# A two-layer decoder on one core: the order of weight preparation in the Strassen pairs, an input tile ahead of the memory jobs, and more attention steps in the first half of an output part

## The chip, the cores and the metric

The kernel runs on one core of a Trainium2 chip. The metric is the device time of one execution in microseconds (us), here the median of three runs; less is better.

## What is computed

A decoder trunk of two layers over x (1024 positions by D = 1024), with a memory of 256 rows. Cut to what matters:

```python
for l in range(2):
    h = rms_norm(x, norm_gains[l, 0])
    z = h @ w_in[l]                              # 768 main + 256 memory columns
    if l == 0:
        y_main = pool_mixer(z[..., :768], w_pool[l], pool_scale[l])
    else:
        y_main = dilated_mixer(z[..., :768], positions, shared)   # 3 groups of 4 heads, softmax over groups
    y_mem = memory_attn(z[..., 768:], mem, mem_norm[l], w_mem_kv[l])
    y = jnp.concatenate([y_main, y_mem], axis=-1) @ w_out[l]
    x = x + rms_norm(y, norm_gains[l, 1])
    h = rms_norm(x, norm_gains[l, 2])
    gu = h @ w_gate_up[l]                        # 2 x 2816 columns
    x = x + rms_norm((silu(gu[..., :2816]) * gu[..., 2816:]) @ w_down[l], norm_gains[l, 3])
    if l == 0:
        shared = build_shared_kv(x, positions, kv_norm, w_kv)
```

`pool_mixer` averages over windows of 2, 4, 8 and 16 positions and multiplies by `w_pool`; `memory_attn` has 4 heads over the 256 memory rows; `dilated_mixer` is a sliding window of 128 keys at dilations 1, 4 and 16. All inputs are float32.

## The kernel before

**Arithmetic.** Every float32 product is three matmuls: each operand is split into a high part (`..H`, a rounding copy on ACT) and a low part (`..L`, the difference, on DVE or POOL), and TensorE adds high x high, low x high and high x low. Activations lie with D on the partitions, in 8 tiles (k) of 128, and the 1024 positions are two halves of 512, so a typical matmul is 128x512.

**Jobs.** `plan_jobs` (L106) lists the jobs in TensorE's order: per layer `in` (input tiles), `mem` (keys and values of the memory), `pool` or `kv`, `out`, `ffn` (the first 4 of 22 hidden tiles, by halves), `st` (the other 18, a **pair** each of a gate and an up tile, computed with 7 Strassen-Winograd products of 4 k x 3 = 12 matmuls, 84 in all), and `down` (32). `region` gives each job's weights a slot in SBUF, `banks` its PSUM banks. A weight comes by a DMA on SP's queue, which issues in order (L2461), gets its gain and high part (`weight_hi`, L1004, ACT) and its low part (`weight_lo`, L1578 on DVE, L2347 on POOL).

**Queues.** Each engine's instruction order is written out by hand in one function per engine and tied together by semaphores: a wait holds all that stands behind it on that engine. Steps of attention (scores L803, transposes L787, values L777 on TensorE; exp L1111, normalising L1117 on ACT; several on DVE) are laid between the matmuls of jobs at the k that `HOOKS` names. Sums over D for the norms are TensorE steps `("col", s, h)` (L688, column sum of squares) and `("row", s, h)` (L697, spread of the inverse root to all partitions); `("mcol",)`, `("mrow",)` are the memory's, `("mv", l, a)` its value transposes (L741, copied by ACT at L1087).

**Pairs.** For pair q, DMA brings four raw tiles into `SR` (1 MB); DVE (layer 0, `st_add`, L1877 to L1880) or POOL (layer 1, L2429 to L2432) forms four sums. ACT makes high parts of the raw tiles (`st_raw_hi`, L1252) and of the sums (`st_sum_hi`, L1257) in `SH`, DVE the low parts `SL` (L1887, L1894). Between these, DVE combines the products of the running pair (u2 L1900, c11 L1906, u3 L1911, L1917 and L1918, c21 L1922, c12 L1927, L1950) and ACT does `p1_copy` (L1279) and silu (L1263 after c11, L1269 after c12). `pe.wait_ge(st_lo, 2 * (q + 1))` opens each pair.

**Weights prepared in advance.** During the first 16 pairs of layer 0, 24 later weights are prepared and written back to HBM: one or two per pair, `prepared(f)` L163. SP loads `VR` (L2469), ACT scales it by its gains and copies its high part (`keep_weight`, L1141, L1144), POOL makes the low part `VL` (L2390), SP writes `w_keep` (L2476, L2479). ACT's part of a pair in layer 0:

```python
p1_copy(q)
if l == 0:
    silu_first(q)
    for i in prepared(f):
        keep_weight(i)
if f < NF - 1:
    st_raw_hi(q + 1)
    st_sum_hi(q + 1)
```

**Other places.** In layer 1, `out` is done in two parts of four k (part 0 beside the last attention steps). The three groups' outputs are weighted against each other per pair of head tiles: `combine(0)`, `combine(1)` on ACT (L1490 to L1496), `combine_last` on DVE, low parts by `split_low` (L1814). Part 1 is added onto part 0 by `add_y` (L1848); `residual` (L1630) adds the input, after y was multiplied by its inverse root: for y of layer 1's mixer this multiplication is POOL's `y_norm` (L2422). Then come x's squares (`accumulate`, L1613), `BH`, `BL` (L1641 low), and `scale_x` (L1075).

## Time and profile before

| what | value |
|---|---|
| three runs | 2398.61, 2398.93, 2392.47 us; median 2398.61 |
| the profiled execution's own time | 2402.4 us |
| its span in the profile | 2400.4 us |
| mean clock that TensorE was granted | 0.955 of full speed |
| instructions | 25623, of which TensorE 9718 matmuls |
| chain that ended last | PE 70%, DVE 12%, ACT 9%, issue 5%, DMA 3% |

A row of a timeline gives an instruction's start, its length, engine, line, operation with tiles as out<-in, and in brackets how long the engine was idle before it and what released it. A waits row names the engine and line that waited, and for whose result. PE is TensorE, PEld its weight loads, DVE VectorE, ACT ScalarE, POOL GpSimd, SPq the queue of DMAs that SyncE issues.

### The profile page before, as it was taken

The page shows a single profiled execution, that of the slowest core. Times are in us where ns is not written, and L with a number is a line of the kernel's source. Part 1 is how long each engine was busy: PE and PEld are TensorE (multiplying, and loading weights), DVE is VectorE, ACT ScalarE, POOL GpSimd, SP SyncE. Part 2 cuts the span into 40 slices and gives each one's busy share as a digit, 9 for nine tenths or more (in the row PEclk, how much of TensorE's full clock was granted, in tenths as well). Part 3 has the DMA queues.
Part 4 walks back from the last instruction along what each step waited for, and adds up shares of the span by engine and source line. Part 5 has one row for each costly group of instructions (what it writes and reads, how often), then busy time and mean ns, then how long its engine had stood idle before and what let it go on. Part 6 is the DMA issues. An engine that isn't in the chain of part 4 may idle for free.

```text
span 2400.4 us, 25623 instructions
## 1 busy us (share of the span) xinstructions
PE 2202.2 (92%) x9718; PEld 1766.8 (74%) x9718; DVE 1264.6 (53%) x1901; ACT 944.5 (39%) x1575; POOL 328.0 (14%) x198
## 2 busy tenths in 40 slices
PE   6897999888888999998999997979799999999996
PEld 5675888776767778887777765657578888878885
DVE  6354375655565643525344445466656666672442
ACT  5335352434344433322444446653542222242421
POOL 3432100112111000000000014022222222200000
PEclk8998999999899999998999999989899999999998
DMA  4202232344444635554111101004212222263543
GB/s 160 73 14 90 88 121 75 142 184 149 179 148 173 222 117 199 163 174 182 53 64 43 59 30 36 19 17 154 75 53 79 79 79 82 94 216 97 197 132 104
DMA packets 83210, 265.10 MB, mean 110 GB/s; under 512 B 9360, under 2 KB 10640, under 8 KB 77840
## 3 DMA queue, kind: packets, MB, share of 16 engines
q1 hardware_dynamic: 66960, 234.10, 27.8%
q10 hardware_dynamic: 16128, 29.37, 3.6%
q8 instruction: 77, 1.26, 0.2%
q14 instruction: 45, 0.37, 0.0%
HBM read 195.14 MB, written 68.29 MB: 110 GB/s over the span
## 4 chain that ended last, share of the span: by engine, by line
PE 70%; DVE 12%; ACT 9%; issue 5%; DMA 3%; SPq 1%; POOL 0%; ACTq 0%; DVEq 0%
PE PS L662 8%; PE PS L875 7%; PE PS L877 7%; PE PS L876 7%; PE PS L663 7%; PE PS L665 7%; PE PS L895 6%; PE PS L897 6%; PE PS L896 6%; PE PSC L803 3%; ACT VR L1141 2%; PE PO L777 2%; DVE SL L1894 2%; PE PTR L787 1%; ACT VH L1144 1%
## 5 line engine op out<-in xcount | busy, mean ns | idle before, releaser
L895 PE MATMUL PS<-IH,DH 128*128 128x512 f32 x704 | 276.6, 393 | 6.5 <-DVE IL L1975 6.0
L897 PE MATMUL PS<-IH,DL 128*128 128x512 f32 x704 | 275.3, 391 | 0.0
L896 PE MATMUL PS<-IL,DH 128*128 128x512 f32 x704 | 275.3, 391 | 0.0
L875 PE MATMUL PS<-BH,SH 128*128 128x512 f32 x432 | 179.1, 415 | 54.7 <-DVE SL L1894 51.6
L875 PE MATMUL PS<-BHT,SH 128*128 128x512 f32 x576 | 225.8, 392 | 0.0
L876 PE MATMUL PS<-BLT,SH 128*128 128x512 f32 x576 | 224.2, 389 | 0.0
L877 PE MATMUL PS<-BHT,SL 128*128 128x512 f32 x576 | 224.2, 389 | 0.0
L876 PE MATMUL PS<-BL,SH 128*128 128x512 f32 x432 | 176.7, 409 | 0.0
L877 PE MATMUL PS<-BH,SL 128*128 128x512 f32 x432 | 176.7, 409 | 0.0
L895 PEld LDWEIGHTS PS<-IH,DH 128*128 128x128 f32 x704 | 132.9, 189 | 36.7 <-DVE IL L1975 8.5
L897 PEld LDWEIGHTS PS<-IH,DL 128*128 128x128 f32 x704 | 133.0, 189 | 27.9
L896 PEld LDWEIGHTS PS<-IL,DH 128*128 128x128 f32 x704 | 133.0, 189 | 27.5
L875 PEld LDWEIGHTS PS<-BH,SH 128*128 128x128 f32 x432 | 85.8, 199 | 79.6 <-DVE SL L1894 61.8
L1578 DVE TENSOR_TENSOR DL<-DR,DH 128x1408 fp32r<-128x1408 f32 x64 | 103.8, 1624 | 73.0 <-ACT DH L1004 73.0
L662 PE MATMUL PS<-XH,WH 128*128 128x512 f32 x320 | 138.8, 434 | 0.0
L663 PE MATMUL PS<-XL,WH 128*128 128x512 f32 x320 | 128.7, 402 | 0.0
L875 PEld LDWEIGHTS PS<-BHT,SH 128*128 128x128 f32 x576 | 109.4, 190 | 23.0
L876 PEld LDWEIGHTS PS<-BLT,SH 128*128 128x128 f32 x576 | 109.4, 190 | 23.0
L1613 DVE TENSOR_TENSOR SS<-SS,SCR 128x512 f32<-128x512 f32 x28 | 19.4, 691 | 202.6 <-ACT SCR L1031 202.6
L877 PEld LDWEIGHTS PS<-BHT,SL 128*128 128x128 f32 x576 | 108.1, 188 | 23.0
L662 PE MATMUL PS<-BH,WH 128*128 128x512 f32 x256 | 104.7, 409 | 20.9 <-DVE WL L1578 13.4
L2390 POOL TENSOR_TENSOR VL<-VR,VH 128x1024 fp32r<-128x1024 f32 x24 | 57.9, 2411 | 470.4 <-ACT VH L1144 470.4
(281 smaller groups left out, 4645.2 us busy)
## 6 DMA issues: line engine op xcount, KB each, us to landing
DR<-in_wdn SPq DMA_DIRECT2D x64, 704.0 KB, 4.1
SR<-in_wst SPq DMA_DIRECT2D x36, 1024.0 KB, 4.8
IR<-inner SPq DMA_DIRECT2D x88, 256.0 KB, 4.9
WR<-in_w SPq DMA_DIRECT2D x36, 512.0 KB, 4.6
inner<-TP SPq DMA_DIRECT2D x36, 512.0 KB, 2.6
VR<-in_w SPq DMA_DIRECT2D x24, 512.0 KB, 4.1
w_keep<-VH SPq DMA_DIRECT2D x24, 512.0 KB, 3.7
w_keep<-VL SPq DMA_DIRECT2D x24, 512.0 KB, 4.6
```

Source lines behind the costliest of these rows:

```text
L662: MM(out[h], wh[:, i, :], rh(h, k), start=(i == 0), stop=False)
L663: MM(out[h], wh[:, i, :], rl(h, k), start=False, stop=False)
L665: ins = MM(out[h], wl[:, i, :], rh(h, k), start=False, stop=last)
L803: MM(score_bank(a)[:, 0:nk], QF[rows, t, P * n:P * (n + 1)], keys, start=True, stop=True).then_inc(scored, 1)
L875: MM(BANK[bank], SH[b][:, w, c], BH[t][:, k, :], start=(k == 0), stop=False)
L876: MM(BANK[bank], SH[b][:, w, c], BL[t][:, k, :], start=False, stop=False)
L877: ins = MM(BANK[bank], SL[b][:, w, c], BH[t][:, k, :], start=False, stop=(k == 3))
L895: MM(bank, wh[:, i, :], IH[r][:, :], start=(k == 0), stop=False)
L896: MM(bank, wh[:, i, :], IL[r][:, :], start=False, stop=False)
L897: ins = MM(bank, wl[:, i, :], IH[r][:, :], start=False, stop=(k == NF - 1))
L1578: V.tensor_tensor(lo(j), raw(j), as_f32(hi(j)), ALU.subtract).then_inc(w_lo_dve, 1)
L2390: G_.tensor_tensor(VL[i % NV][:, :, :], VR[i % NV][:, :, :], as_f32(VH[i % NV][:, :, :]), ALU.subtract).then_inc(v_lo, 1)
```

## The change

- **Opening, layer 0.** The job `in` of tile `POOL_IN[0]` = 3 stands ahead of the four `mem` jobs on TensorE, in the loads and in the preparation of weights, and holds PSUM banks 4 and 5; the `mem` jobs take banks 6, 0, 1, 6. The column and row steps of the first norm lie in it (k = 3, 4 and 7), `mcol` and `mrow` in the memory jobs 0 and 1. SP loads weights only up to job `mem` 3 before it writes `mem_keep` (L2597). ACT squares x before it touches the memory. The later input jobs have 4, 5, 5, 5, 5 steps for 4 each in six.
- **Pairs, layer 0.** ACT's order becomes p1_copy, first `keep_weight`, `st_raw_hi`, `silu_first`, `st_sum_hi`, second `keep_weight`.
- **Junction.** `RSTDM` is reloaded at down job 13; the transposes of memory values lie in the job `in` 7 of half 1 (k = 6) rather than half 0 (k = 4).
- **Attention and out part 0, layer 1.** Four steps in each of the 8 jobs of the first half, one in each of the second (before: 21 and 19). `combine` on ACT is cut into single pieces, and `combine(1)` with `combine_last` stands earlier.
- **Residual and FFN start, layer 1.** `y_norm` leaves POOL, DVE does the multiplication inside `residual`. The `ffn` weights have slots of their own (`2 * f + j`), in space that part 0 of `out` used, and are prepared earlier. `("col", s_x, 1)`, `("row", s_x, 1)` lie in `ffn` job (1, 0, 0) at k = 0 and 4 rather than in (1, 0, 1) at 3 and 7.
- Slots of layer 1's pairs and down jobs are counted from the other parity (`pair_slot`).

```diff
+            run += [Job("in", 0, POOL_IN[0])]
             run += [Job("mem", 0, m, gain=8) for m in range(4)]
-            run += [Job("in", 0, m) for m in POOL_IN]
+            run += [Job("in", 0, m) for m in POOL_IN[1:]]
...
-        jobs += [Job("ffn", l, (f, j), halves=(h,), tag=h, slot=wide(2 * f + j),
+        jobs += [Job("ffn", l, (f, j), halves=(h,), tag=h, slot=2 * f + j if l else wide(2 * f + j),
...
-            HOOKS[J[("out", 1, m, (0, 0))]] = (1, 2, 3) if m < 5 else (1, 3)
-            HOOKS[J[("out", 1, m, (0, 1))]] = (0, 1, 2, 3) if m < 2 else (1, 3) if m < 7 else (1,)
+            HOOKS[J[("out", 1, m, (0, 0))]] = (0, 1, 2, 3)
+            HOOKS[J[("out", 1, m, (0, 1))]] = (1,)
...
-            memory_job(0, 0, hook=at_k({6: [("col", 0, 0), ("col", 0, 1)]}))
-            memory_job(0, 1, hook=at_k({4: [("row", 0, 0), ("row", 0, 1)], 7: [("mcol", 0, 0)]}))
-            memory_job(0, 2, hook=at_k({6: [("mrow", 0, 0)]}))
+            job(J[("in", 0, POOL_IN[0], None)], xh, xl,
+                hook=at_k({3: [("col", 0, 0)], 4: [("col", 0, 1)], 7: [("row", 0, 0), ("row", 0, 1)]}))
+            memory_job(0, 0, hook=at_k({1: [("mcol", 0, 0)]}))
+            memory_job(0, 1, hook=at_k({3: [("mrow", 0, 0)]}))
+            memory_job(0, 2)
             memory_job(0, 3)
...
-                              (1, 0, 1): {3: [("col", s_x, 1)], 7: [("row", s_x, 1)]}}
+                              (1, 0, 0): {0: [("col", s_x, 1)], 4: [("row", s_x, 1)]}}
...
                     p1_copy(q)
+                    ready = prepared(f) if l == 0 else ()
+                    if len(ready):
+                        keep_weight(ready[0])
+                    if f < NF - 1:
+                        st_raw_hi(q + 1)
                     if l == 0:
                         silu_first(q)
-                        for i in prepared(f):
-                            keep_weight(i)
                     if f < NF - 1:
-                        st_raw_hi(q + 1)
                         st_sum_hi(q + 1)
+                    if len(ready) > 1:
+                        keep_weight(ready[1])
...
-                if r != 3:
-                    V.tensor_tensor(y, y, RSTD[:, c], ALU.mult).then_inc(y_normed[h], 1)
+                V.tensor_tensor(y, y, RSTD[:, c], ALU.mult).then_inc(y_normed[h], 1)
...
-                    if h and m >= 2:
-                        combine_last(m - 2)
+                    if (h, m) == (0, 7):
+                        combine_last(0)
+                        combine_last(1)
+                    if h and m in (1, 2, 4, 6):
+                        combine_last((2, 3, 4, 5)[(1, 2, 4, 6).index(m)])
+                    if h and m == 7:
+                        combine_last(6)
+                        combine_last(7)
+                        split_low(7, 22)
...
-            y_norm(0)
-            y_norm(1)
...
-            loads_to(J[("in", 0, POOL_IN[2], None)])
+            loads_to(J[("in", 0, POOL_IN[1], None)])
```

**The order in a layer-0 pair on ACT**, one with two preparations (`VR`, `VH` are the weight being prepared, `SR`, `SH` raw tiles, sums and their high parts, `SCR` p1). Before:

```order
L1279 ACTIVATE SCR_71<-PS 128x512 [waits c21_done,st_mm]
L1263 ACTIVATE TP_91<-TP_91 128x512 [waits c11_done]
L1141 ACTIVATE VR_192<-VR_192,GN 128x128 [waits v_loaded1]
L1141 ACTIVATE VR_192<-VR_192,GN 128x128 x7
L1144 ACTIVATE VH_198<-VR_192 128x1024 [waits v_gained]
L1141 ACTIVATE VR_193<-VR_193,GN 128x128 [waits v_loaded2]
L1141 ACTIVATE VR_193<-VR_193,GN 128x128 x7
L1144 ACTIVATE VH_199<-VR_193 128x1024 [waits v_gained]
L1252 ACTIVATE SH_204<-SR_200 128x1536 [waits st_loaded0]
L1257 ACTIVATE SH_204<-SR_200 128x2048 [waits st_added]
L1269 ACTIVATE TP_91<-TP_91 128x512 [waits c12_done]
```

After:

```order
L1293 ACTIVATE SCR_71<-PS 128x512 [waits c21_done,st_mm]
L1154 ACTIVATE VR_192<-VR_192,GN 128x128 [waits v_loaded1]
L1154 ACTIVATE VR_192<-VR_192,GN 128x128 x7
L1157 ACTIVATE VH_198<-VR_192 128x1024 [waits v_gained]
L1266 ACTIVATE SH_204<-SR_200 128x1536 [waits st_loaded0]
L1277 ACTIVATE TP_91<-TP_91 128x512 [waits c11_done]
L1271 ACTIVATE SH_204<-SR_200 128x2048 [waits st_added]
L1154 ACTIVATE VR_193<-VR_193,GN 128x128 [waits v_loaded2]
L1154 ACTIVATE VR_193<-VR_193,GN 128x128 x7
L1157 ACTIVATE VH_199<-VR_193 128x1024 [waits v_gained]
L1283 ACTIVATE TP_91<-TP_91 128x512 [waits c12_done]
```

The first preparation and the raw conversion (128x1536) moved ahead of the silu that waits for c11, the second preparation behind the conversion of the sums (128x2048).

**The opening on TensorE**, around the first column sum (`SS` squares, `XHA` x's high part, `MH` the memory's). Before, it lies in a memory job:

```order
L729 MATMUL PSC<-ML_64,WH_167 128x256
L730 MATMUL PSC<-MH_66,WL_141 128x256
L688 MATMUL PX<-CN,SS 128x1 [waits ss0_done]
L688 MATMUL PX<-CN,SS 128x1 x3
L688 MATMUL PX<-CN,SS 128x1 [waits px_free,ss0_done]
L688 MATMUL PX<-CN,SS 128x1 x3
L728 MATMUL PSC<-MH_66,WH_167 128x256
L729 MATMUL PSC<-ML_64,WH_167 128x256
L730 MATMUL PSC<-MH_66,WL_141 128x256
L728 MATMUL PTR<-MH_66,WH_168 128x256 [waits w_lo_pool]
```

After, it lies in the inserted input job, between its matmuls:

```order
L672 MATMUL PSC<-XHA,WL_141 128x512
L672 MATMUL PTR<-XHA,WL_141 128x512
L695 MATMUL PX<-CN,SS 128x1 [waits ss0_done]
L695 MATMUL PX<-CN,SS 128x1 x3
L669 MATMUL PSC<-XHA,WH_167 128x512
L670 MATMUL PSC<-XLA,WH_167 128x512
L669 MATMUL PTR<-XHA,WH_167 128x512
L670 MATMUL PTR<-XLA,WH_167 128x512
L672 MATMUL PSC<-XHA,WL_141 128x512
```

**Layer 1's mixer residual on DVE**, first half (`YOA` is y, `WL` a low part of an `ffn` weight). Before:

```order
L1848 TENSOR_TENSOR YOA<-YOA,PO 128x512 [waits mm_done,y_first]
L1630 SCALAR_TENSOR_TENSOR YOA<-YOA,GN,TP_91 128x512 [waits x_back0,y_normed0]
L1641 SCALAR_TENSOR_TENSOR BL_229<-YOA,GN,BH_221 128x512 [waits x_hi0]
L1630 SCALAR_TENSOR_TENSOR YOA<-YOA,GN,TP_91 128x512 [waits x_back1,y_normed0]
L1641 SCALAR_TENSOR_TENSOR BL_229<-YOA,GN,BH_221 128x512 [waits x_hi0]
L1848 TENSOR_TENSOR YOA<-YOA,PS 128x512 [waits mm_done,y_first]
L1578 TENSOR_TENSOR WL_143<-WR_117,WH_169 128x1024 [waits w_hi]
L1630 SCALAR_TENSOR_TENSOR YOA<-YOA,GN,TP_92 128x512 [waits x_back2,y_normed0]
L1641 SCALAR_TENSOR_TENSOR BL_230<-YOA,GN,BH_222 128x512 [waits x_hi0]
L1630 SCALAR_TENSOR_TENSOR YOA<-YOA,GN,TP_91 128x512 [waits x_back0,y_normed0]
L1641 SCALAR_TENSOR_TENSOR BL_230<-YOA,GN,BH_222 128x512 [waits x_hi0]
```

After:

```order
L1606 RECIPROCAL RC<-RC 128x4 [waits px_free]
L1601 TENSOR_TENSOR WL_142<-WR_116,WH_168 128x1024 [waits w_hi]
L1881 TENSOR_TENSOR YOA<-YOA,PTR 128x512 [waits mm_done,y_first]
L1648 TENSOR_TENSOR YOA<-YOA,RSTD 128x512 [waits px_free]
L1652 SCALAR_TENSOR_TENSOR YOA<-YOA,GN,TP_91 128x512 [waits x_back0,y_normed0]
L1648 TENSOR_TENSOR YOA<-YOA,RSTD 128x512
L1652 SCALAR_TENSOR_TENSOR YOA<-YOA,GN,TP_91 128x512 [waits x_back1,y_normed0]
L1663 SCALAR_TENSOR_TENSOR BL_229<-YOA,GN,BH_221 128x512 [waits x_hi0]
L1648 TENSOR_TENSOR YOA<-YOA,RSTD 128x512
L1652 SCALAR_TENSOR_TENSOR YOA<-YOA,GN,TP_92 128x512 [waits x_back2,y_normed0]
L1663 SCALAR_TENSOR_TENSOR BL_229<-YOA,GN,BH_221 128x512 [waits x_hi0]
```

Each L1652 (before L1630) has a multiplication by `RSTD` ahead of it on DVE, and the low parts of weights have left the stretch.

## Rows read from the trace of the kernel before

**Rows 1.** the page's busy us (share of the span) xinstructions

```profile
PE 2202.2 (92%) x9718; PEld 1766.8 (74%) x9718; DVE 1264.6 (53%) x1901; ACT 944.5 (39%) x1575; POOL 328.0 (14%) x198
```

**Rows 2.** what TensorE waited for, whole span: us in total, times, longest

```profile
PE PS L875 <- DVE SL L1894: 51.6, 16, 4.9
PE PO L777 <- ACT PT L1111: 22.1, 9, 7.2
PE PS L662 <- DVE WL L1578: 13.4, 3, 9.9
PE PS L662 <- DVE CL L1814: 11.1, 2, 8.9
PE PX L688 <- DVE SS L1605: 7.0, 1, 7.0
PE PSC L803 <- ACT VM L1087: 5.9, 1, 5.9
PE PX L741 <- DVE MV L1692: 4.7, 1, 4.7
```

**Rows 3.** windows: length, busy us of PE PEld DVE ACT POOL; PEclk, DMA, GB/s

```profile
412.36:791.64 379.28, 327.71 (x1346) 264.30 (x1344) 211.39 (x238) 161.73 (x295) 57.86 (x24) 0.94 0.44 163
1807.42:2110.00 302.58, 302.58 (x1336) 250.56 (x1335) 191.37 (x191) 81.03 (x68) 82.63 (x64) 1.00 0.24 87
44.58:72.44 27.86, 20.08 (x121) 18.69 (x122) 8.56 (x12) 7.83 (x13) 10.21 (x5) 0.81 0.45 156
1668.67:1788.31 119.64, 96.49 (x403) 76.85 (x403) 80.06 (x84) 59.26 (x80) 20.07 (x12) 0.91 0.23 81
```

**Rows 4.** timeline, two pair starts: start, us, engine, line, operation [idle <- releaser]

```profile
433.07 0.50 PE L875 MATMUL PS<-BH,SH 128*128 128x512 f32 x1 [1.50 <-DVE SL L1894]
457.33 0.79 PE L875 MATMUL PS<-BH,SH 128*128 128x512 f32 x1 [4.93 <-DVE SL L1894]
```

**Rows 5.** timeline of ACT in the pair from 433.07, which has two weight preparations

```profile
436.12 0.60 ACT L1279 ACTIVATE SCR<-PS 128x512 f32<-128x512 f32 x1 [0.45 <-PE PS L877]
...
442.82 2.44 ACT L1141 ACTIVATE VR<-VR,GN 128x128 f32<-128x128 f32 x8
...
449.69 1.47 ACT L1252 ACTIVATE SH<-SR 128x1536 fp32r<-128x1536 f32 x1
451.06 1.90 ACT L1257 ACTIVATE SH<-SR 128x2048 fp32r<-128x2048 f32 x1
```

**Rows 6.** DVE in the same pair; L1887 over the kernel (ns, min/median/max)

```profile
441.56 0.69 DVE L1906 TENSOR_TENSOR TP<-SCR,PS 128x512 f32<-128x512 f32 x1 [2.03 <-PE PS L877]
...
455.00 2.28 DVE L1894 TENSOR_TENSOR SL<-SR,SH 128x2048 fp32r<-128x2048 f32 x1
...
L1887 DVE TENSOR_TENSOR SL<-SR,SH x36: 1750/1756/2700, 399.0 to 2107.4; 128x1536 fp32r<-128x1536 f32 x36
```

**Rows 7.** `VL` on POOL, `VR` loads on SP's queue, their us to landing

```profile
425.58 2.41 POOL L2390 TENSOR_TENSOR VL<-VR,VH 128x1024 fp32r<-128x1024 f32 x1 [167.29 <-ACT VH L1144]
...
466.62 3.23 SPq L2469 DMA_DIRECT2D VR<-in_w  x2
...
VR<-in_w SPq DMA_DIRECT2D x24, 512.0 KB, 4.1
```

**Rows 8.** opening: SP's first write of memory, ACT's weight behind it

```profile
59.67 0.33 SPq L2597 DMA_DIRECT2D mem_keep<-MH  x1
...
70.76 1.06 ACT L1004 ACTIVATE WH<-WR 128x1024 fp32r<-128x1024 f32 x1 [9.29 <-DMA WR<-in_w]
```

**Rows 9.** residual and y_norm over the kernel: ns min/median/max, first and last start

```profile
L1630 DVE SCALAR_TENSOR_TENSOR YOA<-YOA,GN,TP x32: 741/752/1780, 282.4 to 1724.4; 128x512 f32<-128x512 f32 x32
...
L2422 POOL TENSOR_TENSOR YOA<-YOA,RSTD x16: 1282/1726/1747, 1647.1 to 1711.7; 128x512 f32<-128x512 f32 x16
```

**Rows 10.** timeline, layer 1's FFN start: ACT's scalings, TensorE's column sum

```profile
1729.86 5.00 ACT L1075 ACTIVATE YOA<-YOA,GN 128x512 f32<-128x512 f32 x8
...
1744.03 0.94 PE L688 MATMUL PX<-CN,SS 128*128 128x1 f32 x8
```

More of the change, by code:

```diff
@@ L594, in build @@
         HOOKS = {}
-        for m in range(NMT):
-            HOOKS[J[("in", 0, m, None)]] = (1, 3, 5, 7)
+        for n, m in enumerate(POOL_IN):
+            HOOKS[J[("in", 0, m, None)]] = () if n == 0 else (4, 5, 6, 7) if n == 1 else (1, 2, 4, 5, 7)
         first_stage_job = J[("kv", 1, stage_tile(0), None)]
@@ L827, in _, with hook @@
                 j = J[("in", 0, m, None)]
-                def hook(i, first=n == 0, places=HOOKS[j]):
-                    if first and i == 0:
+                if n == 0:
+                    continue
+                def hook(i, first=n == 1, places=HOOKS[j]):
+                    if first and i == 2:
                         memory_values(0, 0)
@@ L1163, in _ @@
                     weight_hi(1)
+            weight_hi(2)
+            for k in range(KT):
+                square0(k)
             act.wait_ge(tables_in, MEM_IN)
@@ L1190, in _ @@
                 j = J[("in", 0, m, None)]
-                if n == 0:
+                if n == 1:
                     memory_values(0)
-                ahead(j)
+                if n:
+                    ahead(j)
                 for _ in HOOKS[j]:
@@ L1462, in _ @@
             sub_layer(0)
-            for k in range(6):
-                residual(2, 1, k)
-            memory_values(1)
-            for k in range(6, KT):
+            for k in range(KT):
                 residual(2, 1, k)
@@ L1471, in _ @@
             norm_row(4, 1)
+            memory_values(1)
             for k in range(4, KT):
@@ L1478, in swap_quarter, with combine @@
                 A(T[1][r:r + 32, :], PS[j % 2][q:q + 32, :], ACT.Copy).then_inc(swapped, 1)
-            def combine(pair, stage):
+            def combine(pair, stage, g=None):
                 tiles = [2 * g + pair for g in range(3)]
-                if stage == 0:
-                    for g, t in enumerate(tiles):
-                        act.wait_ge(cmb_diff, 3 * pair + g + 1)
-                        A(QF[:, t, :], QF[:, t, :], ACT.Exp).then_inc(cmb_exp, 1)
-                elif stage == 1:
+                if stage == "exp":
+                    act.wait_ge(cmb_diff, 3 * pair + g + 1)
+                    A(QF[:, tiles[g], :], QF[:, tiles[g], :], ACT.Exp).then_inc(cmb_exp, 1)
+                elif stage == "inverse":
                     tmp = MX[:, :] if pair == 0 else T[3]
@@ L1493, in combine @@
                 else:
-                    for g, t in enumerate(tiles):
-                        act.wait_ge(cmb_out, 3 * pair + g + 1)
-                        A(CH[:, t, :], OF[:, t, :], ACT.Copy).then_inc(c_hi, 1)
+                    act.wait_ge(cmb_out, 3 * pair + g + 1)
+                    A(CH[:, tiles[g], :], OF[:, tiles[g], :], ACT.Copy).then_inc(c_hi, 1)
             def split_memory(m):
@@ L1765, in _, with pooled_input @@
             query0(7)
+            def pooled_input(n):
+                j = J[("in", 0, POOL_IN[n], None)]
+                dve.wait_ge(mm_done, j + 1)
+                if n == 0:
+                    dve.wait_ge(pads_zero, 3)
+                    for h in range(2):
+                        ins = V.tensor_tensor(T[0][:, HALF[h]], BANK[banks(j)[h]], RSTD[:, HALF[h]], ALU.mult)
+                    ins.then_inc(in_scaled, 1)
+                else:
+                    V.tensor_tensor(T[0], PS[j % 2][:, :], RSTD[:, :], ALU.mult).then_inc(in_scaled, 1)
+            pooled_input(0)
             for m in range(4):
@@ L2274, in combine_last @@
                 else:
-                    for n, t in enumerate(tiles):
-                        split_low(t, 18 + n + 1)
-                    split_low(7, 22)
+                    split_low(tiles[part - 5], 18 + part - 4)
             for n in range(19):
@@ L2362, in _ @@
             pool.wait_ge(x0_lo, KT)
-            gain(POOL_JOBS[0])
-            weights_to(first + 3)
+            weight_lo(POOL_JOBS[0])
+            done[0] += 1
+            pool.wait_ge(ss0_done, KT)
+            gain(POOL_JOBS[1])
+            weights_to(J[("in", 0, POOL_IN[3], None)])
             pool.wait_ge(pads_zero, 3)
@@ L2416, in _ @@
             weights_to(NJ)
-            def y_norm(h):
-                pool.wait_ge(px_free, px_at[("row", 5, h)])
-                for k in range(KT):
-                    G_.tensor_tensor(YO[h][:, k, :], YO[h][:, k, :], RSTD[:, HALF[h]],
-                                     ALU.mult).then_inc(y_normed[h], 1)
             def st_add(q):
-                b = SR[q % 2]
+                b = SR[pair_slot(q)]
                 pool.wait_ge(*st_seen(q))
```

117 lines of the change are left out of this document (61 added, 56 removed).

## The prediction

> **What bounds the kernel now.** I read the page's head and busy shares first: one TensorE, busy 2202.2 us, 92% of the span, and no other engine that computes over 53% [rows 1]. So the time is TensorE's matmuls, plus TensorE's idle time, plus what its lower clock costs behind each idle stretch. The next view is therefore the list of what TensorE waited for [rows 2]: the first line is one wait, 16 times, before L875, the first matmul of a Strassen pair, for L1894, DVE's low part of the eight sums (`SL`). It is 51.6 us in all; the next one, attention's 22.1 for `PT`, is less than half of it. The third view prices it: the 16 pair starts of layer 0 are spread over 379.28 us, TensorE idle for 51.6 of them and its clock at 0.94; the layer-1 pairs run in 302.58 us with no idle time at clock 1.00 [rows 3]. There 1336 matmuls take 302.58 us, 0.2265 us each, so a pair of 84 matmuls takes **19.02 us** where nothing stops it; in layer 0 it takes 379.28 / 16 = **23.70 us**.
>
> Why is `SL` late? The timelines of one pair show it, T = 433.07 its first matmul [rows 4 to 6]. ACT copies p1 at T+3.05 and then waits for DVE's c11 (T+8.49) to do silu. Only behind that come two weight preparations (`keep_weight`, 442.82 to 449.69, 3.43 each), then the conversions of the next pair's raw tiles (1.37 until the next one starts) and of its sums (1.90). DVE takes the low parts behind these, the last of them L1894 from T+21.93 to T+24.21, and the next pair starts at T+24.26, after 4.93 of idle time. A pair with one preparation ends the same chain one preparation sooner, and its successor waits 1.50 [rows 4]; eight of each make 51.4.
>
> **Term by term, against the profiled execution (2402.4 us, 3.8 above the runs' median of 2398.61).**
>
> *Pairs (ACT's order).* One preparation and the raw conversion move in front of silu, into the time in which ACT idled for c11; the second preparation goes behind the sum conversion. In the same pair: p1 copied by T+3.65, first preparation to T+7.1, raw conversion to T+8.5 (ACT never waits for its DMA now), c11 ends T+9.2, silu some 0.6 later. DVE makes the sums in four operations (to T+12.0 at c11's 0.69 each) and forms u3 until T+12.6, then L1887 (1.75 unhindered) to T+14.3. ACT's sum conversion goes from T+12.0 to T+13.9. DVE's two sums of products, then L1894 (2.28): `SL` is done at T+17.8. It is wanted at T+19.02, a reserve of 1.2. If nothing is late, 16 x (23.70 − 19.02) = 74.9 goes, of which 51.6 is idle time and 23.3 slow clock (1.46 a pair). Moved too: POOL's low part `VL` of the first preparation, 2.41 long, now begins at T+7.1 rather than at T+13.2 (425.58, in a pair that starts at 412.36), and `w_keep`'s writes with it. L1887 shows what company costs: 2700 against a median of 1756 ns [rows 6, 7]. Add that 0.95 to the chain and it ends at T+18.7, still 0.3 early. I take **−73**; bounds −74.9 (all) and −58 (a gap near 1 us stays in every pair).
>
> By the Trainium skill ("SBUF — State Buffer", section "SBUF: two separate sides") a DVE operation with two SBUF inputs and a GpSimd operation share a port pair as an exclusive lock, held for the whole instruction. The long L1887 agrees in direction, since it lost 0.95 beside `VL`. By that page a DVE operation could lose up to a whole `VL`, 2.41, and then `SL` ends at T+20.2 and 1.2 a pair stays: 19 us less gain. That is rival 1's mechanism.
>
> *Opening (an input job ahead of the memory jobs).* From the column sum that waited 7.0 for DVE's `SS` to the first memory scores that waited 5.9 for `VM`, 27.86 us pass with TensorE busy 20.08 at clock 0.81 [rows 2, 3]. The inserted job gives DVE and ACT its length of 48 matmuls: both waits go (12.9), with 1.9 of smaller gaps (27.86 − 20.08 − 5.9) and 5.3 of slow clock (0.19 x 27.86): 20. New is that the next job's weight lies behind the three writes of memory on SP's queue: now from the first write at 59.67 to ACT's use of the weight at 70.76 it is 11.1 us, and ACT idles 9.29 for it [rows 8]. With the write at about 57.3 (an estimate: the memory's row step is reached 2.4 sooner) the weight lands at 68.4, high part 1.1 and low part 2.4 behind; TensorE is out of prepared work at about 64.5 and idles 7.5, plus 1.6 of clock. Row steps that now stand close behind their column steps cost about 2.2. Together 20 − 11.3, **−8** rounded down; bounds −3 and −12.
>
> *Junction.* The transposes of memory values wait 4.7 for `MV` [rows 2]; they move a half job later. The column sum that follows them is then waited for instead, about half of it: **−2.5**; bounds 0 and −8. The reload of rstd goes to an idle queue place and is costed at nothing; its cover is the down jobs.
>
> *Attention and out part 0.* Thirty-two steps instead of 21 lie in the first half, eight in the second, so the combination of pair 1 is ready before part 1 asks for it. The wait for `CL` (11.1 in two) goes, and 1.4 of clock as behind a pair's gap: **−12.5**; bounds −5 (the shorter spacing of the steps gives some back as waits for `PT`, which is 22.1 already) and −17. Combination 0 in single pieces between steps shortens some of those 22.1: **−2**; bounds 0 and −5.
>
> *Residual and FFN start, layer 1.* From 1668.67 to 1788.31, 119.64 us, all that is not matmul at full clock is at most 119.64 − 403 x 0.2265 = 28.3 (23.2 idle, 5.2 slow clock in the 96.49 busy) [rows 3]. It is the three waits for L1578's `WL` (13.4 [rows 2]) and smaller ones. The weights of the FFN are prepared earlier because out part 0's space is free, so `WL` is no wait. POOL's y_norm (16, median 1726 ns [rows 9]) becomes 16 DVE operations of some 0.75 (no row shows it on DVE; L1630 of that width has median 752 ns): 12 us more of DVE, but POOL no longer stretches L1630 up to 1780. What is late next: the column sum of y's second half, 2.4 (bounds 0 and 6.0, eight such operations); the column sum of x's second half, which waited for nothing at 1744.03 [rows 10] and is now asked 33 matmuls (7.5 us) earlier, 6.0 (0 and 7.5); its row sum behind ACT's eight scalings of 5.00 [rows 10], 3.4 (0 and 5.0). 28.3 − 11.8: **−16.5**; bounds −8 and −24. Slot numbers of layer 1's pairs and down jobs only change parity: nothing.
>
> Sum: −73 − 8 − 2.5 − 12.5 − 2 − 16.5 = −114.5, so 2287.9 for a profiled run, and on the median **2284 us**.
>
> **Rivals.** *1. Half of the pair gain.* The early `VL` or the silu/c11 interlock leaves the eight two-preparation pairs where one-preparation pairs stand now: 1.5 + 1.46 each, 8 x 2.96 = 23.7. For it: the reserve of only 0.3 to 1.2. Against: layer 1's pairs have the same chain without preparations and no gap. **2307**, chance 0.13. *2. Only the pairs gain.* Outside them each removed wait is taken over by another (weight behind `mem_keep`, `PT`, column sums); 39.0 of the gain (8 + 14.5 + 16.5) is void: **2323**, chance 0.07. *3. More goes.* The waits that I added (11.8 at the FFN, about 8 of the opening's 11.3) do not come about: **2264**, chance 0.09. *4. Slower.* The preparation now stands ahead of the raw conversion, so ACT's wait for its weight `VR` holds the next pair. The two loads issue at 466.62, that is 9.3 after their pair's start, for 3.23, and land 4.1 later [rows 7]: T+16.6. They are used in the next pair, at T+19.0 + 3.65 = T+22.7, and 1.2 of reserve stands behind. The rival decides from a landing at about T+31, 14.5 us later, where 7.2 idle a pair (16 x 7.2 = 115) eats the whole gain; at 8.3 a pair it is 2284 + 16 x 8.3 = **2417**. Only 44% of the DMA time is used there [rows 3]: chance 0.02.
>
> **Numbers.** Forecast 0.68, the rest as above, 0.01 unnamed. The range 2262 to 2310 holds the forecast with its bounds, rival 3 and rival 1; rival 2 and 4 lie outside. Changes within 0.3% (7 us) are what this measurement can't tell from none; every case but rival 4 lies far below: faster 0.97, same 0.01, slower 0.02.
>
> **What would show it.** Right: no line L875 <- `SL` in the waits, pairs of 19.0 us at clock 1.00 in layer 0; ACT's second preparation behind the sum conversion; the opening's `SS` and `VM` waits gone, and one of some 7 us for a low weight part in their place; layer 1's pairs start some 114 us sooner, since every term lies ahead of them. Wrong: gaps of 1 us or more at the pairs with two preparations (rival 1), new waits in the place of those for `CL` and `WL`, as long as they were (rival 2), or idle time of ACT before `VR` (rival 4).

## The result, and the profile after

The changed kernel takes **2282.39 us** (median of four runs, 2281.26 to 2292.21) against 2397.72 us before (four runs): a ratio of 0.9532, 95% interval 0.9502 to 0.9562. The forecast was 2284. The profiled execution took 2281.26 us, with a span of 2278.9 us, against 2402.4 and 2400.4.

The head of the page, busy us and share of the span by engine:

```profile
PE 2158.3 (95%) x9718; PEld 1738.4 (76%) x9718; DVE 1254.2 (55%) x1918; ACT 947.2 (42%) x1575; POOL 303.9 (13%) x182
```

TensorE lost 122 us of span and 44 us of busy time (2202.2 in [rows 1]): most of what went was idle time, the rest is the same 9718 matmuls taking less time each. What TensorE waits for now (us in total, times, longest):

```profile
PE PO L784 <- ACT PT L1124: 22.7, 9, 7.2
PE PTR L794 <- DVE PR L1744: 17.7, 13, 2.5
PE PX L695 <- DVE SS L1636: 13.8, 5, 4.9
PE PS L669 <- POOL WL L2381: 7.6, 2, 6.5
PE PS L669 <- DVE CL L1847: 2.4, 3, 1.6
PE PS L888 <- DVE SL L1927: 0.6, 1, 0.6
```

Against [rows 2]: `SL` is down from 51.6 to 0.6; `CL` of `split_low` (L1814 before, L1847 now) is down from 11.1 to 2.4; `WL` on DVE (13.4), `SS` in the opening (7.0), `VM` (5.9) and `MV` (4.7) are gone. New is `WL` on POOL, 6.5 of it in the opening. Up are `SS` of L1636, the sums of squares of later norms, from 1.9 in two to 13.8 in five, and `PR` from 13.6 in eleven to 17.7 in thirteen. The two stretches of pairs, layer 0 and layer 1 (length, busy us of PE, PEld, DVE, ACT, POOL, then PEclk, DMA share, GB/s):

```profile
409.16:753.43 344.27, 343.17 (x1513) 283.55 (x1512) 239.68 (x273) 182.65 (x324) 58.15 (x24) 1.00 0.57 209
1669.61:2012.43 342.82, 342.82 (x1512) 283.87 (x1513) 219.60 (x224) 96.08 (x88) 87.94 (x68) 1.00 0.27 98
```

Eighteen pairs in 344.27 and in 342.82 us, 19.1 and 19.0 each, at clock 1.00 in both layers [rows 3 for before]. ACT, DVE and POOL in the pair that starts at 467.20 and has two preparations:

```profile
470.12 0.60 ACT L1293 ACTIVATE SCR<-PS 128x512 f32<-128x512 f32 x1 [1.36 <-PE PS L890]
470.61 2.44 ACT L1154 ACTIVATE VR<-VR,GN 128x128 f32<-128x128 f32 x8
...
474.04 1.47 ACT L1266 ACTIVATE SH<-SR 128x1536 fp32r<-128x1536 f32 x1
476.28 0.63 ACT L1277 ACTIVATE TP<-TP 128x512 f32<-128x512 f32 x1 [0.76 <-DVE TP L1939]
479.39 1.92 ACT L1271 ACTIVATE SH<-SR 128x2048 fp32r<-128x2048 f32 x1 [2.48 <-DVE SR L1913]
481.21 2.44 ACT L1154 ACTIVATE VR<-VR,GN 128x128 f32<-128x128 f32 x8
```

```profile
475.56 0.69 DVE L1939 TENSOR_TENSOR TP<-SCR,PS 128x512 f32<-128x512 f32 x1 [2.03 <-PE PS L890]
476.16 1.01 DVE L1910 TENSOR_TENSOR SR<-SR 128x512 f32<-128x512 f32 x1
...
479.87 1.75 DVE L1920 TENSOR_TENSOR SL<-SR,SH 128x1536 fp32r<-128x1536 f32 x1
...
482.73 2.28 DVE L1927 TENSOR_TENSOR SL<-SR,SH 128x2048 fp32r<-128x2048 f32 x1
...
485.75 2.08 DVE L1983 TENSOR_TENSOR TP<-TP,TP 128x512 f32<-128x512 f32 x1
```

```profile
474.22 2.41 POOL L2427 TENSOR_TENSOR VL<-VR,VH 128x1024 fp32r<-128x1024 f32 x1 [16.63 <-ACT VH L1157]
484.82 2.45 POOL L2427 TENSOR_TENSOR VL<-VR,VH 128x1024 fp32r<-128x1024 f32 x1 [8.20 <-ACT VH L1157]
```

This is the chain of the forecast, with T = 467.20: preparation 1 from p1's end, raw conversion at T+6.8, silu behind c11, sum conversion at T+12.2, L1927 done at 485.01 = T+17.8, where the forecast had T+17.8. The next pair starts at 486.24, 19.04 after T.

Cut by TensorE's marks in the timelines, the two profiled executions and those of experiments 2, 1, 8 and 11 stand so (us; "to the PT wait" ends at the 5 us wait for `PT` ahead of the out part, [rows 2, 22.1 in all]):

| stretch | before | after | new pair order alone | old pair order | old attention steps | late weights |
|---|---|---|---|---|---|---|
| up to layer 0's pairs | 412.4 | 409.2 | 410.5 | 411.8 | 410.2 | 410.6 |
| its pairs | 420.8 | 344.2 | 344.3 | 421.0 | 344.3 | 344.3 |
| its down jobs | 251.7 | 251.1 | 252.7 | 251.2 | 252.4 | 252.9 |
| layer 1 to the PT wait | 413.7 | 402.6 | 407.2 | 403.6 | 407.7 | 407.4 |
| to layer 1's pairs | 289.7 | 262.4 | 289.6 | 262.7 | 272.9 | 288.3 |
| its pairs | 345.5 | 342.8 | 345.6 | 342.8 | 342.8 | 344.7 |
| the rest | 266.6 | 266.5 | 265.8 | 265.7 | 266.1 | 266.3 |

### The profile page after: what moved, and what is told of

The parts are those of the page before. It is cut to its first block, busy times and chain, and to the rows that moved or that the text cites. A ratio compares the mean times of both kernels' runs of the same rounds, so it can differ in the third digit from the quotient of the medians.

```text
span 2278.9 us, 25627 instructions
## 1 busy us (share of the span) xinstructions
PE 2158.3 (95%) x9718; PEld 1738.4 (76%) x9718; DVE 1254.2 (55%) x1918; ACT 947.2 (42%) x1575; POOL 303.9 (13%) x182
## 4 chain that ended last, share of the span: by engine, by line
PE 81%; DVE 8%; ACT 4%; DMA 3%; issue 3%; SPq 0%; POOL 0%; ACTq 0%; DVEq 0%
PE PS L890 9%; PE PS L888 9%; PE PS L889 9%; PE PS L669 8%; PE PS L670 8%; PE PS L672 7%; PE PS L908 7%; PE PS L909 6%; PE PS L910 6%; PE PSC L812 3%; PE PO L784 2%; PE PTR L794 1%; DMA TP<-x_mid 1%; DVE SS L1636 1%; DVE IL L2008 1%
## 5 line engine op out<-in xcount | busy, mean ns | idle before, releaser
L888 PE MATMUL PS<-BH,SH 128*128 128x512 f32 x432 | 168.3, 389 | 0.6 <-DVE SL L1927 0.6
L889 PE MATMUL PS<-BL,SH 128*128 128x512 f32 x432 | 168.1, 389 | 0.0
L890 PE MATMUL PS<-BH,SL 128*128 128x512 f32 x432 | 168.0, 389 | 0.0
L1636 DVE TENSOR_TENSOR SS<-SS,SCR 128x512 f32<-128x512 f32 x28 | 19.4, 691 | 202.5 <-ACT SCR L1044 202.5
L1734 DVE CUSTOM_DVE_ANT_0 PSC<-PSC,MK 128x128 f32<-128x128 f32 (+1 forms) x88 | 32.2, 366 | 157.1 <-PE PSC L812 156.9
L1271 ACT ACTIVATE SH<-SR 128x2048 fp32r<-128x2048 f32 x36 | 69.1, 1920 | 107.8 <-POOL SR L2462 67.9
```

The source lines that it names most:

```text
L888: MM(BANK[bank], SH[b][:, w, c], BH[t][:, k, :], start=(k == 0), stop=False)
L889: MM(BANK[bank], SH[b][:, w, c], BL[t][:, k, :], start=False, stop=False)
L890: ins = MM(BANK[bank], SL[b][:, w, c], BH[t][:, k, :], start=False, stop=(k == 3))
L1271: A(SH[pair_slot(q)][:, S3:, :], SR[pair_slot(q)][:, S3:, :], ACT.Copy).then_inc(st_hi, 1)
```

## The experiments

**1. The old pair order in the changed kernel.** ACT's part of a pair only:

```diff
-                    ready = prepared(f) if l == 0 else ()
-                    if len(ready):
-                        keep_weight(ready[0])
-                    if f < NF - 1:
-                        st_raw_hi(q + 1)
                     if l == 0:
                         silu_first(q)
+                        for i in prepared(f):
+                            keep_weight(i)
                     if f < NF - 1:
+                        st_raw_hi(q + 1)
                         st_sum_hi(q + 1)
-                    if len(ready) > 1:
-                        keep_weight(ready[1])
```

> The changed kernel with ACT's old order in the layer-0 pairs (silu, all weight preparations, raw conversion, sum conversion), nothing else undone. Theory (this order alone makes SL late): the gaps of 1.5 and 4.9 us in front of L888 come back at 16 pairs, with the slow clock behind them, some 76 us: about 2358 us. Rival (the pairs are freed by other parts too, such as the slots or the opening): clearly less comes back, 2300 to 2340, with gaps of another size.

Measured: 2359.84 us (2357.46 to 2363.29), 77.5 more than the changed kernel. The list of waits has the old row back, with the same numbers:

```profile
PE PS L888 <- DVE SL L1923: 51.6, 16, 4.9
```

**2. The new pair order alone in the kernel before** (the same edit the other way round).

> The kernel before with the new ACT order in the layer-0 pairs and nothing else of the change. Theory: 76 us go, 2398 - 76 = about 2322 us, and the other parts keep their waits (SS 7.0, VM 5.9, CL 11.1, WL 13.4). Rival (parts depend on each other): less than 65 us go.

Measured: 2319.84 us (2315.84 to 2324.16) against 2396.46, 76.6 less. The other stretches are those of before within 2 us, but for the one to the PT wait, 407.2 against 413.7 (below). Undone and done alone give the same size, so the pairs' gain depends on no other part.

**3. Silu ahead of the first preparation.** Only the second preparation keeps its new place:

```diff
+                    if l == 0:
+                        silu_first(q)
                     if len(ready):
                         keep_weight(ready[0])
                     if f < NF - 1:
                         st_raw_hi(q + 1)
-                    if l == 0:
-                        silu_first(q)
-                    if f < NF - 1:
                         st_sum_hi(q + 1)
```

> The changed kernel, but with silu ahead of the first preparation: p1 copy, silu, preparation 1, raw conversion, sum conversion, preparation 2. Only the second preparation is still moved. Chain theory: c11 ends at T+9.0, preparation 1 at T+13.1, raw conversion T+14.6, DVE's L1920 behind POOL's VL until about T+17.3, L1927 until about T+20.5: each of the 16 pairs waits about 1.5 us as a one-preparation pair did before, and with 1.46 of slow clock each it is 16 x 2.96 = 47 us more, about 2329 us. Rival (only two preparations in a row hurt, one does not): no gap, 2282 us.

Measured: 2309.27 us (2305.34 to 2309.98), 26.9 more than the changed kernel and 20 less than the 2329 expected. The waits row, the window of one pair of it, and for comparison two pairs of the kernel before, the first behind a wait of 1.50 and the second behind one of 4.93 (the last three numbers are PEclk, DMA share, GB/s; each window ends with the wait of the next pair):

```profile
PE PS L888 <- DVE SL L1926: 24.1, 16, 1.5
```

```profile
453.00:473.83 20.83, 19.33 (x84) 15.69 (x84) 14.69 (x16) 8.34 (x14) 4.60 (x2) 1.00 0.66 230
```

```profile
433.07:457.33 24.26, 19.33 (x84) 15.69 (x84) 13.32 (x16) 11.85 (x23) 4.81 (x2) 0.97 0.46 170
457.33:480.74 23.41, 21.91 (x85) 17.57 (x85) 13.33 (x16) 8.45 (x14) 2.41 (x1) 0.88 0.47 162
```

The gap is the 1.5 us of the chain, 16 times: that theory stands. The slow clock behind it does not exist: a pair takes 19.33 busy us at clock 1.00 behind a gap of 1.50 (0.3 over 19.02, what stopping and starting costs TensorE), and 21.91 at 0.88 behind one of 4.93. The timeline of the kernel before shows the clock in the matmuls' spacing:

```profile
458.35 0.63 PE L877 MATMUL PS<-BH,SL 128*128 128x512 f32 x1
458.78 0.63 PE L875 MATMUL PS<-BH,SH 128*128 128x512 f32 x1
...
463.18 0.39 PE L877 MATMUL PS<-BHT,SL 128*128 128x512 f32 x1
463.41 0.40 PE L875 MATMUL PS<-BHT,SH 128*128 128x512 f32 x1
```

Behind the gap of 4.93 the starts are 0.43 apart until 462.62, then 0.23: the lower and the higher of the two levels (1.2 and 2.4 GHz), 13 matmuls at 0.2 us more each. So of the 23.3 us that I had put down to the clock, 7 long gaps in that window made 7 x 2.58 = 18, and the stops and starts 16 x 0.3 = 5; the short gaps cost no clock.

The second preparation's move alone thus gives about two thirds of the gain, 50 of 77 us, and the work put ahead of silu the other 27.

**4. Both preparations ahead of the raw conversion.**

```diff
-                    if len(ready):
-                        keep_weight(ready[0])
+                    for i in ready:
+                        keep_weight(i)
...
-                    if len(ready) > 1:
-                        keep_weight(ready[1])
```

> The changed kernel, but with both preparations ahead of the raw conversion. By ACT's chain alone (preparations to T+10.5, raw conversion T+12.0, sum conversion behind the sums at T+12.0) SL is still ready at T+17.8: 2282 us, no gap. If POOL's VL blocks a two-input DVE operation until VL ends, the second VL (T+10.6 to T+13.0) holds DVE's sums until about T+13.9, and SL is ready at about T+19.5: gaps near 0.5 us at the 8 pairs behind two preparations, with slow clock 10 to 16 us more, 2292 to 2298 us.

Measured: 2292.44 us (2289.90 to 2294.12), 10 more; in the profile the pairs take 352.8 us against 344.3. POOL's second `VL`, DVE's second and third sum, and the waits:

```profile
480.52 2.50 POOL L2425 TENSOR_TENSOR VL<-VR,VH 128x1024 fp32r<-128x1024 f32 x1 [1.04 <-ACT VH L1157]
```

```profile
480.07 0.69 DVE L1909 TENSOR_TENSOR SR<-SR 128x512 f32<-128x512 f32 x1
480.80 2.78 DVE L1910 TENSOR_TENSOR SR<-SR 128x512 f32<-128x512 f32 x1
```

```profile
PE PS L888 <- DVE SL L1925: 6.8, 9, 0.8
```

The sum L1910 starts 0.28 behind `VL` and ends at 483.58, that is 0.56 after `VL` ends at 483.02: nearly all of the 0.69 us that it takes alone lies behind `VL`. That is what the lock of the Trainium skill ("SBUF — State Buffer", section "SBUF: two separate sides") says, and the trace agrees with its number: 2.78 us instead of 0.69. ACT's own chain had room for both preparations; what forbids it is POOL's operation that a preparation sets off. The changed order is better because its second `VL` starts at 484.82, 0.19 before `SL` is done, where it stretches L1983 (another 128x512 operation) to 2.08 and nobody waits.

**5. The opening undone** (the job list, the steps' places, and the orders of ACT, DVE, POOL and SP there as in the kernel before).

```diff
-            run += [Job("in", 0, POOL_IN[0])]
             run += [Job("mem", 0, m, gain=8) for m in range(4)]
-            run += [Job("in", 0, m) for m in POOL_IN[1:]]
+            run += [Job("in", 0, m) for m in POOL_IN]
...
```

> The changed kernel with the opening undone (memory jobs ahead of all pooled input tiles, four steps in each of the six, loads and engines as before). By the forecast's term the opening is worth 8 us: 2290 us. By the two traces the pairs of layer 0 start only 3.2 us sooner: 2286 us. The waits SS (7.0) and VM (5.9) return and the waits POOL WL (6.5) and four times PR (1.83) go.

Measured: 2285.25 us (2283.19 to 2286.51), 2.9 more by the medians, but the single times overlap with the changed kernel's, and against the runs of before beside them both have nearly the same ratio (0.9526 with the opening undone, 0.9532 with it). What the opening is worth is therefore not clear of noise, and nothing here shows the 8. In the profile layer 0's pairs start at 411.8, 2.6 later than in the changed kernel's, with `SS` 7.05 and `VM` 5.51 again, and without the waits of 6.49 and 1.83.

**6. The steps of the pooled tiles spread.**

```diff
-            HOOKS[J[("in", 0, m, None)]] = () if n == 0 else (4, 5, 6, 7) if n == 1 else (1, 2, 4, 5, 7)
+            HOOKS[J[("in", 0, m, None)]] = () if n == 0 else (4, 5, 6, 7) if n == 1 else (1, 3, 4, 6, 7)
```

> The changed kernel, the attention steps of the last four pooled input tiles at k = 1, 3, 4, 6, 7 instead of 1, 2, 4, 5, 7. Theory (the second step comes too close behind the first, where DVE still has the pooled tile of the job before, 1.83 us at each of four jobs): those gaps go, about 7.5 us less, 2275 us. Rival (five steps a job are too many for DVE and ACT wherever they lie): the wait moves to k = 4 or 7 and the time stays at 2282 us.

Measured: 2275.98 us (2274.47 to 2278.67), 6.4 less. In the changed kernel's timeline the second step of each of these jobs waits for DVE's `PR` (one of four rows of 1.83 to 2.08):

```profile
116.34 0.44 PE L794 MATMUL PTR<-CN,PR 128*128 128x128 f32 x2 [1.83 <-DVE PR L1744]
```

DVE is then still at the pooled tile of the job before, for whose high part it idles 1.12, and at the scaling of its own:

```profile
111.69 1.23 DVE L1815 TENSOR_TENSOR CL<-TP,CH 128x1024 fp32r<-128x1024 f32 x1 [1.12 <-ACT CH L1200]
112.94 1.22 DVE L1799 TENSOR_TENSOR TP<-PS,RSTD 128x1024 f32<-128x1024 f32 x1
...
114.81 1.48 DVE L1744 TENSOR_SCALAR PR<-PR,RL 128x256 f32<-128x256 f32 x1
```

With one k more between the two steps six waits of 0.47 to 0.85 are left there, 3.8 us in place of 7.6, and the opening is 5.2 shorter (404.0 against 409.2 us up to the pairs), so less slow clock is probably part of it (0.93 from 68 to 240 us, 0.91 in the changed kernel's execution). This is where the opening's forecast gain went: 24 steps that lay four to a job in six jobs now lie in five.

**7. The second pooled tile's weight ahead of the writes of memory.**

```diff
-            loads_to(J[("in", 0, POOL_IN[1], None)])
+            loads_to(J[("in", 0, POOL_IN[2], None)])
             sp.wait_ge(mem_hi, 1)
```

> The changed kernel, the weight of the second pooled tile loaded ahead of the three writes of memory on SP's queue. Theory (the 6.5 us wait for POOL's WL is the load's place in the queue): the wait goes, 6.5 us and up to 1.5 us of slow clock, 2274 to 2276 us. Rival (the load waits for its slot, freed by the first memory job, or ACT and POOL are busy): half or more of the wait stays, 2279 to 2282 us.

Measured: 2277.05 us (2274.44 to 2282.57), 5.3 less, but spread over 8 us, so that the two kernels' single times overlap. The wait of 6.49 at 68.55 is gone in the profile. That execution (2282.57) nevertheless reaches layer 0's pairs at the same time as the changed kernel's: the same `PR` gaps follow, one of 1.21 is new at 75.39, and from 68 to 240 the granted clock is 0.88 where it was 0.91.

```profile
68.00:240.00 172.00, 147.32 (x635) 108.94 (x636) 79.32 (x153) 66.94 (x143) 62.41 (x40) 0.91 0.12 40
```

```profile
68.00:240.00 172.00, 146.87 (x608) 107.59 (x607) 80.83 (x153) 66.10 (x143) 60.92 (x39) 0.88 0.11 40
```

**8. The old attention steps and the old combination** (the steps of the out part, `combine` and `combine_last` as in the kernel before).

```diff
-            HOOKS[J[("out", 1, m, (0, 0))]] = (0, 1, 2, 3)
-            HOOKS[J[("out", 1, m, (0, 1))]] = (1,)
+            HOOKS[J[("out", 1, m, (0, 0))]] = (1, 2, 3) if m < 5 else (1, 3)
+            HOOKS[J[("out", 1, m, (0, 1))]] = (0, 1, 2, 3) if m < 2 else (1, 3) if m < 7 else (1,)
...
```

> The changed kernel with the attention steps of the out part and all of the combination undone (21 steps in the first half, 19 in the second, combination in whole pieces where it was). By the forecast's terms (12.5 + 2) it is 14.5 us slower, by the two traces 13.6: 2296 us, with the wait for CL near 8.9 us back. Rival (the early FFN weights had already covered it): under 5 us slower.

Measured: 2290.48 us (2286.84 to 2298.97), 8.1 more by the medians, with single times that overlap; in the profile the stretch to layer 1's pairs is 10.5 longer (272.9 against 262.4). The wait is back:

```profile
PE PS L669 <- DVE CL L1839: 11.3, 2, 8.9
```

**9. y_norm on POOL again.**

```diff
+                if r != 3:
-                V.tensor_tensor(y, y, RSTD[:, c], ALU.mult).then_inc(y_normed[h], 1)
+                    V.tensor_tensor(y, y, RSTD[:, c], ALU.mult).then_inc(y_normed[h], 1)
...
+                    G_.tensor_tensor(YO[h][:, k, :], YO[h][:, k, :], RSTD[:, HALF[h]],
+                                     ALU.mult).then_inc(y_normed[h], 1)
```

> The changed kernel with layer 1's y_norm on POOL again, as it was before. Theory (POOL's operation shuts a two-input DVE operation out until it ends, so taking it off POOL was worth something): L1652 shows up to 1.8 us again, the starts of the FFN jobs wait for it, and it is 3 to 8 us slower, 2285 to 2290 us. Rival (DVE is what is late there, its waits SS of 3.3 and 4.9 us come from the 12 us of multiplications that it took over): those waits shrink and it is 3 to 8 us faster, 2274 to 2279 us.

Measured: 2282.57 us (2281.07 to 2287.82): no difference that this measurement can tell. In the profile the stretch to layer 1's pairs is 265.8 against 262.4, and the column sum of x's second half waits 7.91 where it waited 4.87:

```profile
1629.89 1.86 PE L695 MATMUL PX<-CN,SS 128*128 128x1 f32 x8 [7.91 <-DVE SS L1636]
```

```profile
1621.99 1.87 PE L695 MATMUL PX<-CN,SS 128*128 128x1 f32 x8 [4.87 <-DVE SS L1636]
```

```profile
L1653 DVE SCALAR_TENSOR_TENSOR YOA<-YOA,GN,TP x32: 735/752/1783, 280.4 to 1626.0; 128x512 f32<-128x512 f32 x32
```

So the rival (DVE's extra work makes `SS` late) is out: with less work on DVE the wait is longer, since L1653 goes up to 1783 ns beside POOL (at most 755 in the changed kernel) and waits 3.6 us for POOL's results. The size, 3 us, rests on one profile, and the medians don't show it; the theory's 3 to 8 us are not shown either.

**10. The norm steps of x's second half one job later.**

```diff
-                              (1, 0, 0): {0: [("col", s_x, 1)], 4: [("row", s_x, 1)]}}
+                              (1, 0, 1): {0: [("col", s_x, 1)], 4: [("row", s_x, 1)]}}
```

> The changed kernel, the column and row steps of x's second half at k = 0 and 4 of FFN job (1, 0, 1) instead of (1, 0, 0), 24 matmuls or 5.4 us later. Theory (the step is only asked too early): the wait SS of 4.9 us goes and nothing else comes, 2277.5 us. Rival (silu and products behind the row step are what is late next): a wait of the same size for TP, and 2282 us or more.

Measured: 2285.62 us (2279.95 to 2286.93), no gain. The 4.9 us wait is gone and stands later, as 2.58 for the row sum (`RC`) and as two waits for `TP`:

```profile
1659.24 0.47 PE L669 MATMUL PS<-BH,WH 128*128 128x512 f32 x1 [0.92 <-DVE TP L1861]
1668.07 0.77 PE L888 MATMUL PS<-BH,SH 128*128 128x512 f32 x1 [3.09 <-DVE TP L1874]
```

The work behind the norm is what is late there; the step's place only chooses who waits.

**11. Layer 1's FFN weights late again** (old slots, and the places of the weights and of `add_y` in ACT's and DVE's order around the residual as before, y_norm still on DVE).

```diff
-        jobs += [Job("ffn", l, (f, j), halves=(h,), tag=h, slot=2 * f + j if l else wide(2 * f + j),
+        jobs += [Job("ffn", l, (f, j), halves=(h,), tag=h, slot=wide(2 * f + j),
...
```

> The changed kernel with layer 1's FFN weights prepared in the old slots and at the old places on ACT and DVE, and with add_y at its old places; y_norm stays on DVE, the norm steps stay where they are now. Theory (the early weights are what the FFN start gained): the wait for DVE's WL near 9.9 us comes back, on top of it DVE has 12 us more to do, and the stretch up to layer 1's pairs is 17 to 27 us longer, 2299 to 2309 us. Rival (the gain came from y_norm and the norm steps): under 5 us slower.

Measured: 2311.33 us (2310.0 to 2316.6), 29 more. The waits:

```profile
PE PS L669 <- DVE WL L1602: 11.5, 3, 6.9
PE PS L888 <- DVE TP L1875: 16.9, 1, 16.9
```

`WL` is back with 11.5, as expected; what was not is the 16.9 us at the first pair, for the last product of the FFN: DVE, with y_norm and eight low parts in the same stretch, ends far behind. The stretch to layer 1's pairs is 288.3 long. The kernel before has late weights too, but y_norm on POOL: 289.7, or about 279 if the 10.5 of the old attention steps (experiment 8) are taken off, an estimate. So with late weights y_norm on DVE costs some 9 us, and with early ones nothing (experiment 9): early weights are what makes room on DVE for it.

**12. Edits 6 and 7 together**, a version that beats both kernels.

> The changed kernel with two edits together: attention steps of the pooled input tiles at k = 1, 3, 4, 6, 7, and the second pooled tile's weight loaded ahead of the writes of memory. If the two waits are independent (6.4 and 5.3 us by the medians of the single runs): 2282 - 12 = about 2270 us. If the lower clock that stood behind the second edit alone (0.88 against 0.91 from 68 to 240 us in its profile) came with the 1.84 us gaps, it is gone too, and the full 6.5 us of the weight comes on top of the spread: 2269 us. Rival (the weight's gain is lost again in the steps that follow): 2276 us, as with the spread alone.

Measured: **2267.76 us** (2265.95 to 2269.34), ratio to the kernel before 0.9463 (0.9438 to 0.9488), 14.6 less than the changed kernel. Layer 0's pairs start at 395.9 instead of 409.2. The clock from 68 to 240:

```profile
68.00:240.00 172.00, 151.35 (x665) 112.31 (x664) 82.62 (x156) 71.02 (x149) 64.77 (x42) 0.93 0.12 40
```

The two edits add up: 6.4 and 5.3 alone, 14.6 together, and the 3 more are within what single medians are uncertain by. In the profiles the opening is 5.2 shorter with edit 6 alone and 13.3 with both. That the low clock of experiment 7 (0.88) came with the 1.8 us gaps is not shown: the eight other profiled executions with these gaps have 0.90 to 0.92 in this window, the five without them 0.92 or 0.93, and experiment 7's three other runs were 3.8 to 8.1 us faster than the profiled one.

## Why the prediction was right, term by term

| term | forecast | measured |
|---|---|---|
| pairs | −73 | −76.6 in the two traces; 77.5 and 76.6 in experiments 1 and 2 |
| opening | −8 | −3.2 in the traces; −2.9 by the medians of experiment 5, within noise |
| junction and combination 0 | −2.5 and −2 | −11.1 to the PT wait; 6.5 of it, perhaps all, is the execution |
| attention and out part | −12.5 | −10.5 in experiment 8's trace, 8.1 by its median |
| residual and FFN start | −16.5 | 27.3 − 10.5 = −16.8; −18.7 from the first FFN matmul to the pairs |
| layer 1's pairs | 0 | −2.7 |

*Pairs.* Right in mechanism and chain, and `SL` came at T+17.8 as written. The steps written down add up to T+18.0, since each DVE operation here begins some 0.1 before the last one's recorded end. The ceiling of 74.9 was 2 short, because the window ended at the last of the 16 gaps and left out the 2.6 us of slow clock behind it. The step "slow clock (1.46 a pair)" was a wrong reading: an average over two kinds of boundary, 2.9 behind each long gap (2.6 clock, 0.3 restart) and 0.3 behind the short ones. It made no difference to the sum, since both kinds went, but it mis-sized rival 1 (8 x 2.96, where 8 x 1.8 is measured) and experiment 3. Of rival 1's mechanism little came: the first `VL` meets only the first sum (L1910, 1.01 where the others take 0.69), so being held up costs 0.32 here and not 2.41. In the kernel before `VL` met L1887 in all 16 of these pairs and stretched it to 2.70; of the same operations now (L1920) only the first pair's is stretched. Rival 4's wait came once, in that first pair, where ACT idled 5.21 for `VR` and TensorE 0.63 for `SL`.

*Opening.* The steps "both waits go" and "idles 7.5" for the weight behind the memory's writes held (6.5). What failed is that nothing was set down for five attention steps a job instead of four. Four waits of 1.83 to 2.08 for `PR`, 7.6 in all where such waits had been 1.9, took 5.7 back (experiment 6), so that waits of 13.0 went and 12.2 came. Mis-sized as well is "5.3 of slow clock (0.19 x 27.86)": it prices 7.8 us of idle time too, in which a low clock costs nothing; on the 20.08 busy us it is at most 3.8. The timeline had the rows for the first: DVE's pooled tile at a job's start, and the order's steps at k = 1 and 2.

*Junction.* `MV` 4.7 went and `SS` 3.7 came, so what was gained in waits is 1, not 2.5. The stretch itself is not steady: experiment 2, whose program is that of before there, has 407.2 and not 413.7, and two executions of the changed program have 407.1 and 407.4, no less. So beyond that 1 us no gain of this stretch is shown. Combination 0 gained nothing that is seen: the wait for `PT` behind it is 5.33 and was 4.92.

*Attention.* The wait for `CL` of 8.9 went, as forecast. The term was 2 too large because it took in both waits for `CL` (11.1); the other one stands in layer 0, where this part changes nothing:

```profile
234.19 0.80 PE L662 MATMUL PS<-CH,WH 128*128 128x512 f32 x1 [2.19 <-DVE CL L1814]
```

In the changed kernel it is still 1.64. The denser steps gave nothing back as `PT` and `PR` waits: behind the PT wait and ahead of the FFN these are 8.8 us in the changed kernel's trace and 10.6 in that of before.

*FFN start.* The sum is right, its parts less so. From the first FFN matmul to the pairs, before and after (the columns of [rows 3]):

```profile
1663.47:1788.31 124.84, 100.88 (x421) 80.14 (x421) 85.20 (x91) 62.34 (x83) 20.07 (x12) 0.91 0.26 89
```

```profile
1563.50:1669.61 106.11, 97.69 (x421) 79.99 (x420) 77.64 (x92) 57.97 (x78) 7.43 (x4) 0.94 0.22 76
```

Three waits are left, 8.4 us instead of 11.8: `SS` for y's second half 3.29 (2.4 forecast), for x's second half 4.87 (6.0), the row sum 0.24 (3.4). Against that the 421 matmuls take 2.3 us more than at full clock (421 x 0.2265 = 95.4), for which nothing was set down. Forecast as costing nothing to move, y_norm did cost nothing (experiment 9); on DVE it takes 684 ns (0.75 forecast). The 2.7 us of layer 1's pairs go with the wait of 3.1 for `TP` that stood ahead of them: in the 60 us behind it the clock was 0.95, and is 1.00 now. I had counted the gap and not the clock behind it. Its price is not steady: behind 3.09 in experiment 10 the pairs took 1.4 us more, behind 16.9 in experiment 11 1.9.

The sum was 6.6 short in the profiled executions (2287.9 against 2281.3). (Rival 2's 39.0 left out the junction's 2.5; that changes nothing here.) The two medians, 2284 against 2282.4, differ less, because the profiled execution of before was itself in a long stretch from layer 1's start to the `PT` wait. That they differ by only 1.6 is partly luck: the pairs gave some 4 more than forecast, the opening 5 and attention 2 to 4 less.

## What to carry to other kernels

An engine that waits for a late result, with work of the next block queued behind it, is a place to look for first: moving some 5 us of independent work in front of the wait gave 27 us here, and moving work that nobody waits for behind the conversions that TensorE does wait for gave 50. No other part of the change came near it. Before moving work forward, follow what it sets off on the other engines, since POOL's subtraction and not ACT's time decided where the second preparation may stand. When a job's steps are made denser, look at what the step's other engines do at the job's border.
